# Wide products for forty blocks of the second gated layer and for the gated linear unit of the last mixer

## The chip, the core and the metric

The kernel is one program on one core of a Trainium2 chip. The metric is its time on the device in microseconds, as the median of several runs; a profiled execution stands beside it.

## What is computed

Two blocks of layers work on 256 tokens of width 2048. The first has two gated layers, the second four mixers (SSD, fox, MLA, S5), each with a layer norm behind it. The change touches the second gated layer and the last mixer. In the second gated layer (`last`), only keys and values are made for the 256 context tokens as well; everything else is for the 256 tokens alone:

```python
        proj = h @ w_in[layer]
        u, v_sgu, za, q, k, v, zb = jnp.split(proj, SPLIT_POINTS, axis=-1)
        q = apply_axial_rope(rms_norm(split_heads(q, N_Q_HEADS), q_norm_w[layer]), cos, sin)
        ...
        attn = blocked_gqa(q, k_all, v_all)
        sgu = chunk_sgu(u, v_sgu, w_sgu[layer], b_sgu[layer], v_norm_w[layer])
        y = jnp.concatenate([sgu * jax.nn.silu(za),
                             merge_heads(attn) * jax.nn.silu(zb)], axis=-1) @ w_out[layer]
```

The last mixer multiplies twice by a 2048 x 2048 matrix behind its state space part, the first time as a gated linear unit (GLU):

```python
    y = jax.nn.gelu(y)
    y = y * jax.nn.sigmoid(y @ w_glu.astype(f32) + b_glu.astype(f32))
    y = y * jax.nn.silu(z.astype(f32))
    return y.astype(h.dtype) @ w_out
```

## The kernel before

**Products in parts.** Every weight and every activation is split into a high part in the format of TensorE's quick float32 product and the low rest. A product of weight W and activation A is W_hi A_hi + W_hi A_lo + W_lo A_hi. The activations stand in `act_parts`, both parts of it, feature by feature (128 features to a tile, 256 tokens wide).

**The stream of weights.** Weights come from HBM in units of 128 x 1024 (8 tiles, 512 KB) through a ring of four (`raw`, `w_hi`, `w_lo`). SyncE starts the DMA of a unit as soon as TensorE has multiplied the unit four before it. ScalarE makes `w_hi` (line 510), VectorE `w_lo` (line 517), and TensorE waits for `w_lo` of a unit before its first tile.

**Blocks.** A `Block` makes 128 output features: 16 tiles, two units, into one PSUM bank. A narrow block has three products of 256 columns in a tile (lines 584, 586, 588). A wide block (`wide`) has two: line 581 multiplies the high weights with both parts of the activation at once, 512 columns, into both halves of the bank; line 588 adds the low weights' product to the first half. Somebody has to add the halves then. Where VectorE takes the result, it does so with one more add. Where ScalarE takes it, VectorE first adds the halves into `norm_root` (`add_halves`, line 620), and ScalarE takes from there. Before the change, all 65 input blocks of the fox mixer and 15 of the 16 output blocks of each mixer are wide; the gated layers, the MLA's and S5's input blocks and the GLU are narrow.

**The order.** `flow` writes out the instructions of a stage block by block, in slots. In slot g ScalarE and VectorE first split units until they are two units (`AHEAD`) past block g, with the side work of the stage in between or behind; then ScalarE takes block g. In the gated layers (`between` is true) the side work stands between the two units of a slot; in the S5 mixer both units come first and the side work behind them. Every engine works its queue in order, so an instruction that waits holds up all behind it.

**Second gated layer.** `LAYER_ORDER` gives the blocks: k, k, v, v, then q and zb of eight heads in turn, then vg and u of eight groups in turn, then eight za. Forty of them, all but k and v, have only the 256 tokens. The banks 0 and 1 take turns (`banks=2`). The attention of a head and the statistics of a group are side work of later slots.

**GLU.** Its 16 blocks follow the 32 input blocks of the S5 mixer. Of the first four the first halves (8 tiles) are multiplied ahead (`LEAD["s5_glu"]`), so that their own slots have one unit each. In a slot, behind the `w_lo`, VectorE does `gate` (line 3374) and `low_out` (3378) of the block before and `halve` (3369) of this one; ScalarE does `high_out` (3297) of the block before and then takes the block with a sigmoid (3442). `gate` waits for the take, `high_out` for `gate`, `low_out` for `high_out`:

```python
                if g - first_glu - 1 in range(KT - 1):
                    gate(dve, g - first_glu - 1)
                    low_out(dve, g - first_glu - 1)
                if g - first_glu in range(KT):
                    halve(dve, g - first_glu)
```

Of the kernel before, what the change touches and what calls it, by code (L numbers as in the profile page):

```python
# [19 lines left out]
KT = D // P  # L20
# [27 lines left out]
LEAD = dict(gate_in1=2, fox_in=3, mla_in=3, s5_in=2, s5_glu=4)  # L48
# [115 lines left out]
LAYER_ORDER = [(name, i) for name in "kv" for i in range(N_KV)] \  # L164
# [198 lines left out]
def halves_first(blocks, n):  # L363

    return [Part(block, block.kt // 2) for block in blocks[:n]] + blocks
# [7 lines left out]
def build(nc, ins, out):  # L373
    with ExitStack() as ctx:
# [304 lines left out]
        def act_rhs(width_of_block, offset=0, first=0):  # L679

            def rhs(k, part, w):
                a = (first + k) * width_of_block + offset
                return act_parts[:, part, a:a + w]
            return rhs
# [756 lines left out]
        def layer_flow(layer, before, behind):  # L1441

            last = layer == DEPTH - 1
# [492 lines left out]
            def wait_result(pe, kk):  # L1936
                if kk < 8:
                    pe.wait_ge(head_low.sem, head_low.at(kk + 1))
                else:
# [1 line left out]
            takes = dict(k=take_k, v=take_v, q=take_q, vg=take_vg, za=take_za, u=take_u, zb=take_zb)  # L1941
            blocks = [Block(KT, TT if name in "kv" else width, both, takes[name](i),
                            wait=None if (name, i) != LAYER_ORDER[0] else before.wait_tile,
                            shape=in_halves if last and name in "kv" else None) for name, i in LAYER_ORDER]
            for i in range(0 if last else QUARTERED):
                blocks[i].place = i
            blocks = halves_first(blocks, lead) if last else quarters_first(blocks, QUARTERED)
# [4 lines left out]

        first_input, second_input, tokens_in = FirstInput(), SecondInput(4, 5), Tokens()
        layer_flow(0, first_input, second_input)
        layer_flow(1, second_input, tokens_in)

        def add_scaled(dve, ps, b):
            if b == KT - 1:
                return dve.scalar_tensor_tensor(out=xT[:, b, :], in0=xT[:, b, :], scalar=ALPHA, in1=ps,
                                                op0=ALU.mult, op1=ALU.add)  # L1960
            ordered = order["vector"]
            dve.scalar_tensor_tensor(out=xT[:, b, :], in0=xT[:, b, :], scalar=ALPHA, in1=ps[:, 0, :],
                                     op0=ALU.mult, op1=ALU.add).then_inc(ordered.sem, 1)
            dve.wait_ge(ordered.sem, ordered.step())
            return dve.tensor_tensor(xT[:, b, :], xT[:, b, :], ps[:, 1, :], ALU.add)  # L1965
# [1164 lines left out]
        def s5():  # L3130
# [36 lines left out]
            last = KT - 1  # L3167
# [273 lines left out]
            def take_glu(b):  # L3441
                return lambda act, ps: act.activation(glu[:, b, :], ps, ACT.Sigmoid, bias=param("b_glu", b, b + 1))

            def wait_y(b):

                def wait(pe, kk):
                    if b == 2 and kk == 0:
                        pe.wait_ge(drive_read.sem, drive_read.at(KT))
                    if b == 0:
                        pe.wait_ge(y_low.sem, y_low.at(kk + 1))  # L3450
                return wait

            def wait_out(pe, kk):
# [2 lines left out]
                            wait=None if (name, k) != S5_ORDER[0] else norms[2].wait_tile) for name, k in S5_ORDER]  # L3456
            blocks = halves_first(blocks, lead)
            blocks += halves_first([Block(KT, T, act_rhs(T, first=KT), take_glu(b), wait=wait_y(b) if b in (0, 2) else None,
                                          place=(0, 1, 4, 5)[b] if b < 4 else None) for b in range(KT)], LEAD["s5_glu"])
            blocks += [Block(KT, T, act_rhs(T), lambda dve, ps, b=b: add_scaled(dve, ps, b), "dve",  # L3460
                             None if b else wait_out, wide=b < KT - 1) for b in range(KT)]
            norms.append(LayerNorm(3, 4, 5, out=False))
            flow(blocks, banks=2, before=norms[2], behind=norms[3], out_at=first_glu + KT, tensor_side=tensor_side, scalar_early=scalar_early, vector_side=vector_side,
                 gpsimd_side=gpsimd_side, scalar_first=scalar_first, vector_first=vector_first)
        s5()
        stage(tensor=norms[3].begin_tensor, scalar=lambda act: norms[3].begin_scalar(act, lambda i: None),
              vector=lambda dve: norms[3].begin_vector(dve, lambda i: None))
# [178 lines left out]
```

## Time and profile before

| | us |
|---|---|
| median of 3 runs | 3359.23 |
| lowest and highest | 3356.72, 3362.01 |
| profiled execution | 3363.07 |
| its span in the trace | 3360.9 |
| TensorE, VectorE, ScalarE busy | 3255.5, 2271.2, 1819.1 |

The span is what the trace covers; the execution has 2.2 us around it. Matmul ends are modelled, so distances are read from start to start. The second gated layer's forty blocks run from about 910 to 1189 us, the GLU's 16 blocks from about 3166 to 3247 us.

### The profile page before, as it was taken

What the parts mean: (1) busy time and instruction counts of PE and PEld (TensorE: products, weight loads), DVE (VectorE), ACT (ScalarE), POOL (GpSimd) and SP (SyncE); (2) the same over time, 40 slices, a digit from 0 to 9 for tenths busy, and PEclk for the clock granted to TensorE, in tenths of its full rate; (3) what the DMA queues carried; (4) which work ended last, traced back from release to release, by engine and by line L of the source; (5) the groups of instructions that cost most, each with busy time, mean ns of one, the idle gap of its engine ahead of it and who ended that gap; (6) DMA issues with size and microseconds to landing.
All of it is one profiled execution on the core that took longest, in us unless ns stands there. A gap on an engine that the chain in (4) does not pass through costs nothing.

```text
span 3360.9 us, 54980 instructions
## 1 busy us (share of the span) xinstructions
PE 3255.5 (97%) x22635; PEld 2905.6 (86%) x22635; DVE 2271.2 (68%) x3092; ACT 1819.1 (54%) x2888; POOL 482.2 (14%) x740
## 2 busy tenths in 40 slices
PE   7999999999899999999999999999999999899997
PEld 3688888788799999999999877888879998899996
DVE  2688889733555556766766676766676655899866
ACT  2344544232577646676775355555546564687644
POOL 0011111111000000000000014877120000322001
PEclk9999999999999999999999999999999999999999
DMA  9855566732244555555555546666545445455454
GB/s 344 286 184 182 181 210 221 285 111 94 84 136 151 176 182 190 195 182 199 184 187 166 184 151 197 219 217 208 178 158 167 148 135 177 150 170 168 158 183 143
DMA packets 175321, 608.44 MB, mean 181 GB/s; under 512 B 21888, under 2 KB 21920, under 8 KB 173408
## 3 DMA queue, kind: packets, MB, share of 16 engines
q1 hardware_dynamic: 145440, 495.54, 43.7%
q0 software_dynamic: 28624, 105.72, 9.1%
q8 instruction: 180, 2.95, 0.4%
q10 hardware_dynamic: 1008, 3.67, 0.3%
q14 instruction: 69, 0.57, 0.1%
HBM read 596.27 MB, written 8.57 MB: 180 GB/s over the span
## 4 chain that ended last, share of the span: by engine, by line
PE 83%; DVE 6%; ACT 4%; DMA 4%; issue 2%; SPq 0%; DVEq 0%; ACTq 0%
PE psum_all L588 24%; PE psum_all L584 18%; PE psum_all L586 18%; PE psum_all L581 12%; DMA raw<-in_stream 2%; DVE w_lo L517 2%; ACT w_hi L510 1%; DMA mod_early<-in_stream 1%; PE psum_all L1564 1%; PE psum_all L1531 1%; PE psum_all L751 1%; DMA mod_late<-in_stream 1%; DVE ln_d L1101 1%; PE psum_all L3202 1%; PE psum_all L3232 0%
## 5 line engine op out<-in xcount | busy, mean ns | idle before, releaser
L588 PE MATMUL psum_all<-act_parts,w_lo 128*128 128x256 f32 (+1 forms) x6704 | 2007.2, 299 | 0.0
L517 DVE TENSOR_TENSOR w_lo<-raw,w_hi 128x1024 fp32r<-128x1024 f32 x866 | 1071.7, 1245 | 704.6 <-ACT w_hi L510 702.3
L584 PE MATMUL psum_all<-act_parts,w_hi 128*128 128x256 f32 (+1 forms) x4464 | 1407.1, 315 | 37.3 <-DVE act_parts L978 13.8
L586 PE MATMUL psum_all<-act_parts,w_hi 128*128 128x256 f32 (+1 forms) x4464 | 1377.7, 309 | 0.0
L588 PEld LDWEIGHTS psum_all<-act_parts,w_lo 128*128 128x128 f32 x6704 | 1281.5, 191 | 41.5
L510 ACT ACTIVATE w_hi<-raw 128x1024 fp32r<-128x1024 f32 x866 | 911.9, 1055 | 687.2 <-DMA raw<-in_stream 685.4
L584 PEld LDWEIGHTS psum_all<-act_parts,w_hi 128*128 128x128 f32 x4464 | 856.4, 192 | 108.7 <-issue 43.3
L586 PEld LDWEIGHTS psum_all<-act_parts,w_hi 128*128 128x128 f32 x4464 | 857.5, 192 | 43.0 <-issue 3.4
L581 PE MATMUL psum_all<-act_parts,w_hi 128*128 128x512 f32 x2240 | 801.2, 402 | 14.6 <-DVE w_lo L517 7.1
L581 PEld LDWEIGHTS psum_all<-act_parts,w_hi 128*128 128x128 f32 x2240 | 422.5, 189 | 123.5 <-issue 10.3
L879 DVE SCALAR_TENSOR_TENSOR xT<-mod_late,small,xT 128x1024 f32<-128x1024 f32 x210 | 256.6, 1280 | 8.2 <-DMA mod_late<-in_stream 6.2
L814 POOL DMA_DIRECT2D mod_late<-in_stream x128 | 67.7, 529 | 568.2 <-DVE xT L879 375.6
L1072 POOL TENSOR_TENSOR ln_acc<-xT 128x256 f32<-128x256 f32 x8 | 5.9, 734 | 586.5 <-DVE xT L1965 586.5
L1072 POOL TENSOR_TENSOR ln_acc<-ln_acc,xT 128x256 f32<-128x256 f32 x44 | 48.2, 1095 | 222.3 <-DVE xT L1965 222.3
L751 PE MATMUL psum_all<-mod_early,s_silu 128*32 128x512 f32 x256 | 48.3, 678 | 24.9 <-DMA mod_early<-in_stream 24.7
L2382 DVE SCALAR_TENSOR_TENSOR conv_acc<-conv_x,params,conv_acc 128x255 f32<-128x255 f32 x144 | 69.3, 481 | 3.5
L1913 DVE SCALAR_TENSOR_TENSOR xT<-psum_all,modulation,xT 128x256 f32<-128x256 f32 x32 | 15.4, 483 | 81.5 <-PE psum_all L588 81.5
L2457 POOL DMA_DIRECT2D acs_rows<-ssd_acs x1 | 0.6, 556 | 467.3 <-DVE ssd_red L2374 467.3
L2462 POOL DMA_DIRECT2D ssd_seg<-acs_rows x8 | 4.3, 533 | 404.1 <-PE psum_all L2259 401.8
L2315 ACT ACTIVATE ssd_seg<-ssd_seg,ssd_src 128x128 f32<-128x128 f32 x192 | 58.6, 393 | 0.8 <-DMA ssd_seg<-acs_rows 0.8
L2471 ACT ACTIVATE conv_acc<-psum_all,params 128x256 f32<-128x256 f32 x48 | 27.0, 562 | 58.0 <-PE psum_all L588 57.4
L751 PEld LDWEIGHTS psum_all<-mod_early,s_silu 128*32 128x32 f32 x256 | 8.2, 115 | 51.0 <-DMA mod_early<-in_stream 35.7
(499 smaller groups left out, 3398.4 us busy)
## 6 DMA issues: line engine op xcount, KB each, us to landing
raw<-in_stream SPq DMA_DIRECT2D x858, 512.0 KB, 3.3
mod_late<-in_stream POOLq DMA_DIRECT2D x128, 512.0 KB, 4.2
mod_early<-in_stream SPq DMA_DIRECT2D x128, 256.0 KB, 6.3
ssd_seg<-acs_rows POOLq DMA_DIRECT2D x8, 1536.0 KB, 6.6
s_matrices<-s5p_made POOLq DMA_DIRECT2D x16, 384.0 KB, 3.0
raw<-in_stream SPq DMA_DIRECT2D x16, 256.0 KB, 5.1
s_made<-s_matrices POOLq DMA_DIRECT2D x16, 256.0 KB, 3.0
xT<-in_x SPq DMA_DIRECT2D x1, 2048.0 KB, 10.5
```

Of the source, the lines that this page charges most:

```text
L510: act.activation(w_hi[:, n % RING, :], raw[:, n % RING, :], ACT.Copy).then_inc(hi_ready, 1)
L517: dve.tensor_tensor(w_lo[:, n % RING, :], raw[:, n % RING, :], w_hi[:, n % RING, :].bitcast(F32), ALU.subtract).then_inc(lo_ready, 1)
L581: pe.matmul(block.both, w_hi[:, n % RING, cols], block.rhs(kk, BOTH, block.width), start=(kk == 0), stop=False)
L584: pe.matmul(sums, w_hi[:, n % RING, cols], block.rhs(kk, HIGH, block.width), start=(kk == 0), stop=False)
L586: pe.matmul(sums, w_hi[:, n % RING, cols], block.rhs(kk, LOW, block.width), start=False, stop=False)
L588: last = pe.matmul(sums, w_lo[:, n % RING, cols], block.rhs(kk, HIGH, block.width), start=False, stop=(kk == block.kt - 1))
L751: last = pe.matmul(bank[rows, :], s_silu[:, k, :], early_units[early_slot(m)][:, h * 512:(h + 1) * 512], start=(k < 2), stop=(k >= KT - 2))
L814: pool.dma_start(late_units[:, m % LATE_RING, :], ins["stream"][u]).then_inc(late_landed[m % LATE_RING], 16)
L879: dve.scalar_tensor_tensor(out=sums, in0=unit, scalar=s_late[:, k, v:v + 1], in1=sums, op0=ALU.mult, op1=ALU.add).then_inc(late_summed, 1)
L1072: pool.tensor_tensor(acc, acc if b % 8 > 1 else xT[:, b - 1, :], xT[:, b, :], ALU.add) \
L2315: one = act.activation(s, s, ACT.Relu, bias=src_cum[:, g * HG + j, k:k + 1], scale=-1.0)
L2382: dve.scalar_tensor_tensor(out=conv_acc[i % 2][:, back:T], in0=conv_x[i % 2][:, 0:T - back], scalar=conv_col(block, tap), in1=conv_acc[i % ...
```

## The change

The forty blocks without context of the second gated layer and the 16 blocks of the GLU become wide:

```diff
@@ -1941,7 +1941,8 @@
                             wait=None if (name, i) != LAYER_ORDER[0] else before.wait_tile,
-                            shape=in_halves if last and name in "kv" else None) for name, i in LAYER_ORDER]
+                            shape=in_halves if last and name in "kv" else None,
+                            wide=last and name not in "kv") for name, i in LAYER_ORDER]
@@ -3456,7 +3457,7 @@
             blocks += halves_first([Block(KT, T, act_rhs(T, first=KT), take_glu(b), wait=wait_y(b) if b in (0, 2) else None,
-                                          place=(0, 1, 4, 5)[b] if b < 4 else None) for b in range(KT)], LEAD["s5_glu"])
+                                          place=(0, 1, 4, 5)[b] if b < 4 else None, wide=True) for b in range(KT)], LEAD["s5_glu"])
```

Lines behind the first place move down by one (3374 becomes 3375).

TensorE has 896 instructions less. This is a piece of the difference, at the start of the forty blocks, behind a transpose of v (L1506) and a rotation of k (L1499); rows that repeat are left out:

```order
 L1499 MATMUL psum_all<-k_6455,consts 128x256
-L584 MATMUL psum_all<-act_parts,w_hi 128x256
-L586 MATMUL psum_all<-act_parts,w_hi 128x256
-L588 MATMUL psum_all<-act_parts,w_lo 128x256
...
+L581 MATMUL psum_all<-act_parts,w_hi 128x512
+L588 MATMUL psum_all<-act_parts,w_lo 128x256
```

Each tile has one product of 512 columns where it had two of 256.

VectorE in the second gated layer, behind the rotation of the first head's q (L1734, L1736) and at its row maxima (L1758, L1763):

```order
 L1734 TENSOR_TENSOR q_6454<-q_6454,consts 128x256
 L1736 TENSOR_TENSOR q_6454<-q_6454,qk_spin_6462 128x256
-L517 TENSOR_TENSOR w_lo<-raw,w_hi 128x1024 x3
+L517 TENSOR_TENSOR w_lo<-raw,w_hi 128x1024 x2
+L620 TENSOR_REDUCE norm_root<-psum_all 128x256
+L517 TENSOR_TENSOR w_lo<-raw,w_hi 128x1024
 L1758 TENSOR_REDUCE head_stat_0_6463<-psum_all 128x1 x2
 L1763 SCALAR_TENSOR_TENSOR head_stat_0_6463<-head_stat_0_6463 128x2
 L517 TENSOR_TENSOR w_lo<-raw,w_hi 128x1024
+L620 TENSOR_REDUCE norm_root<-psum_all 128x256
```

An add of the halves stands behind the last `w_lo` of each slot.

VectorE in the GLU, between two blocks in its middle, before:

```order
L3369 TENSOR_TENSOR s_z<-s_z,s_u 128x256 [waits taken_by_scalar]
L517 TENSOR_TENSOR w_lo<-raw,w_hi 128x1024 [waits hi_ready] x2
L3374 TENSOR_TENSOR s_glu<-s_glu,s_z 128x256 [waits s5_halved,taken_by_scalar]
L3378 TENSOR_TENSOR act_parts<-s_glu,act_parts 128x256 [waits s5_high2]
L3369 TENSOR_TENSOR s_z<-s_z,s_u 128x256 [waits taken_by_scalar]
```

and after:

```order
L3370 TENSOR_TENSOR s_z<-s_z,s_u 128x256 [waits taken_by_scalar]
L620 TENSOR_REDUCE norm_root<-psum_all 128x256 [waits taken_by_scalar,multiplied]
L517 TENSOR_TENSOR w_lo<-raw,w_hi 128x1024 [waits hi_ready] x2
L3375 TENSOR_TENSOR s_glu<-s_glu,s_z 128x256 [waits s5_halved,taken_by_scalar]
L3379 TENSOR_TENSOR act_parts<-s_glu,act_parts 128x256 [waits s5_high2]
```

The add stands behind gate, split and halve, ahead of the next two `w_lo`. ScalarE's order is the same as before; in the GLU its take (L3442, now L3443) waits for `halves_added` where it waited for `multiplied`, and reads `norm_root` where it read PSUM.

## Rows read from the trace of the kernel before

**Rows 1.** The page's busy time, share of the span and instructions of each engine.
```profile
PE 3255.5 (97%) x22635; PEld 2905.6 (86%) x22635; DVE 2271.2 (68%) x3092; ACT 1819.1 (54%) x2888; POOL 482.2 (14%) x740
```

**Rows 2.** Windows, layer and GLU: busy us (count) of PE, PEld, DVE, ACT, POOL; clock.
```profile
910.00:1189.00 279.00, 279.00 (x2193) 269.18 (x2193) 146.51 (x226) 190.48 (x300) 0.00 (x0) 1.00 0.47 155
3166.00:3247.00 81.00, 81.00 (x685) 80.81 (x674) 51.27 (x75) 41.27 (x60) 0.00 (x0) 1.00 0.53 178
```

**Rows 3.** Timeline of TensorE in the GLU: start, duration, engine, line, operation.
```profile
3176.00 0.28 PE L584 MATMUL psum_all<-act_parts,w_hi 128*128 128x256 f32 x1
...
3178.88 0.28 PE L584 MATMUL psum_all<-act_parts,w_hi 128*128 128x256 f32 x1
```

**Rows 4.** Timeline of TensorE in two output projections with wide tiles.
```profile
2803.66 0.39 PE L581 MATMUL psum_all<-act_parts,w_hi 128*128 128x512 f32 x1
...
2809.21 0.39 PE L581 MATMUL psum_all<-act_parts,w_hi 128*128 128x512 f32 x1
...
3246.92 0.40 PE L581 MATMUL psum_all<-act_parts,w_hi 128*128 128x512 f32 x1
...
3252.57 0.40 PE L581 MATMUL psum_all<-act_parts,w_hi 128*128 128x512 f32 x1
```

**Rows 5.** Timeline of VectorE, then ScalarE, at a halves-add of the fox mixer.
```profile
2102.06 0.68 DVE L620 TENSOR_REDUCE norm_root<-psum_all 128x256 f32<-128x512 f32 x1
...
2102.77 0.42 ACT L2826 ACTIVATE fox_q<-norm_root 128x256 f32<-128x256 f32 x1 [1.91 <-DVE norm_root L620]
2103.09 1.04 ACT L510 ACTIVATE w_hi<-raw 128x1024 fp32r<-128x1024 f32 x1
```

**Rows 6.** Timeline of VectorE in the second gated layer (vg slot, za slots).
```profile
1096.89 1.23 DVE L517 TENSOR_TENSOR w_lo<-raw,w_hi 128x1024 fp32r<-128x1024 f32 x1
...
1175.17 1.23 DVE L517 TENSOR_TENSOR w_lo<-raw,w_hi 128x1024 fp32r<-128x1024 f32 x1 [1.00 <-ACT w_hi L510]
1178.02 1.23 DVE L517 TENSOR_TENSOR w_lo<-raw,w_hi 128x1024 fp32r<-128x1024 f32 x1 [1.62 <-ACT w_hi L510]
```

**Rows 7.** Timeline of ScalarE in the same slots.
```profile
1092.22 0.38 ACT L1902 ACTIVATE u<-psum_all 128x256 f32<-128x256 f32 x1 [1.44 <-PE psum_all L588]
...
1098.64 0.38 ACT L1891 ACTIVATE vg<-psum_all 128x256 f32<-128x256 f32 x1 [0.48 <-PE psum_all L588]
...
1176.57 0.38 ACT L1898 ACTIVATE za<-psum_all 128x256 f32<-128x256 f32 x1 [1.43 <-PE psum_all L588]
...
1179.85 1.06 ACT L510 ACTIVATE w_hi<-raw 128x1024 fp32r<-128x1024 f32 x1 [1.55 <-DMA raw<-in_stream]
```

**Rows 8.** Timeline of VectorE in the GLU: block 0, then block 14.
```profile
3169.88 0.42 DVE L3369 TENSOR_TENSOR s_z<-s_z,s_u 128x256 f32<-128x256 f32 x1
...
3239.95 1.22 DVE L517 TENSOR_TENSOR w_lo<-raw,w_hi 128x1024 fp32r<-128x1024 f32 x1 [1.10 <-ACT w_hi L510]
3241.09 0.42 DVE L3374 TENSOR_TENSOR s_glu<-s_glu,s_z 128x256 f32<-128x256 f32 x1
3241.99 0.43 DVE L3378 TENSOR_TENSOR act_parts<-s_glu,act_parts 128x256 fp32r<-128x256 f32 x1 [0.48 <-ACT act_parts L3297]
3242.33 0.42 DVE L3369 TENSOR_TENSOR s_z<-s_z,s_u 128x256 f32<-128x256 f32 x1
3243.30 1.23 DVE L517 TENSOR_TENSOR w_lo<-raw,w_hi 128x1024 fp32r<-128x1024 f32 x1 [0.55 <-ACT w_hi L510]
```

**Rows 9.** Timeline of ScalarE in the GLU at block 14.
```profile
3241.54 0.42 ACT L3297 ACTIVATE act_parts<-s_glu 128x256 fp32r<-128x256 f32 x1 [1.63 <-DVE s_glu L3374]
3241.86 0.46 ACT L3442 ACTIVATE s_glu<-psum_all,params 128x256 f32<-128x256 f32 x1
3242.22 1.05 ACT L510 ACTIVATE w_hi<-raw 128x1024 fp32r<-128x1024 f32 x1
```

**Rows 10.** Timeline of TensorE at the start of the fox mixer.
```profile
1998.46 0.76 PE L581 MATMUL psum_all<-act_parts,w_hi 128*128 128x512 f32 x1 [4.92 <-DVE act_parts L1158]
```

**Rows 11.** Busy time and granted clock just behind it (columns as in rows 2).
```profile
1999.00:2010.00 11.00, 8.80 (x26) 6.39 (x24) 10.93 (x18) 9.61 (x17) 0.00 (x0) 0.50 0.15 48
```

## The prediction

> **What bounds the kernel now.** I read first the busy shares of the page: TensorE is busy 97% of the span, VectorE 68%, ScalarE 54% [rows 1]. An average doesn't tell what a single stage waits for, so the windows come next: in the second gated layer (910 to 1189 us) TensorE is busy 279.0 of 279 us and VectorE 146.5; in the gated linear unit, GLU below (3166 to 3247), TensorE is busy 81.0 of 81 us, VectorE 51.3, and the clock is 1.00 (2.4 GHz) in both [rows 2]. So both changed stretches go by the rhythm of TensorE's products. But VectorE and ScalarE make the weight halves for them, in program order, in the same queues in which they take the results. So the third view is the timeline of the three engines: what a tile costs TensorE, and how much of a block's time the other two need.
>
> **What a tile costs.** A narrow tile is three products of 256 columns. In the GLU its first product starts at 3176.00 and that of the tile eight later at 3178.88 [rows 3]: 0.360 us a tile, 5.76 us a block of 16. A wide tile (512 and 256 columns) is in this kernel already. Sixteen of them take 3246.92 to 3252.57 us, 0.353 each, and sixteen others 2803.66 to 2809.21, 0.347 each [rows 4]. These are two rhythms that a stretch keeps from its first product on; in the timelines about four tiles in five go by the slower. I take 0.352, so a changed tile gives TensorE 0.008 us; the bounds are 0.0067 and 0.013.
>
> A page of the Trainium skill would give less. "TensorE: Matmul & The Clock Gate", section "Back-to-back issue gap", puts a warm product at its columns through 2.4 GHz plus 2.5 ns, so that two of 256 cost 218 ns and one of 512 costs 216, and a tile would win 0.0026 us. Row and rule disagree here: by the rule a narrow tile is 0.328 us, and the trace has 0.360.
>
> **Second gated layer: 40 blocks, 640 tiles.** TensorE saves 640 x 0.008 = 5.1 us (4.3 to 8.3). Added are 40 halves-adds on VectorE (line 620). One takes 0.68 us, and ScalarE's take starts 0.71 us after the add began, its next instruction 0.32 us after that [rows 5]. 40 x 0.68 = 27 us fit into the 132 us in which VectorE is idle there, so throughput is no question. The order is: VectorE now stands at the add until the block's last product, and ScalarE stands at its take until the add is through; behind them wait the next w_hi and w_lo. In a za block nothing but its 16 tiles is on TensorE. There w_lo starts at 1175.17 and ends at 1176.40, the take starts at 1176.57 and the next w_lo at 1178.02 [rows 6, 7]. The add goes in at about 1176.5, and take, w_hi and w_lo move by some 0.7 us: that w_lo ends at 1179.95. TensorE wants it one block after 1176.4, at 1182.0, so 2 us are left. The second w_hi (1179.85) waits for its DMA, and by then ScalarE is free again: nothing is handed on. The tightest are the vg and u pairs, where ScalarE makes statistics between u's take (1092.22) and the second w_lo (1096.89), the last thing before vg's add: 4.67 + 1.14 + 0.71 = 6.5 us from take to take, where the trace has 6.42 (1098.64) [rows 6, 7]. That hands on 0.1 to 0.3 us, and the u slot behind it, which has no statistics, takes it back. A q and zb pair has TensorE's attention work beside its tiles, so more room. Banks: with two of them, a block needs the bank of the last but one, whose take is late by 0.7 us and has 5.65. I put the loss in the layer at 0, at most 1 us.
>
> **GLU: 16 blocks, 256 tiles.** Here the order is another: in each slot both w_lo come first, then gate, split and halve of the block before (lines 3374, 3378, 3369), and now the add behind these. The steps form a ring over the two engines, read from the starts [rows 8, 9]: last w_lo to gate 1.14 (3239.95 to 3241.09), gate to ScalarE's split 0.45 (3241.54), split to VectorE's 0.45 (3241.99), to halve 0.34 (3242.33). From there on before ScalarE did not wait for it: the take started 0.32 after its split (3241.86), w_hi 0.36 after that (3242.22), w_lo 1.08 later (3243.30), and the second w_lo could follow 1.14 later. The ring before is 1.14 + 0.45 + 0.32 + 0.36 + 1.08 + 1.14 = 4.5 us with two units a slot, under TensorE's 5.76.
> Now the take hangs behind split, halve and add: 1.14 + 0.45 + 0.45 + 0.34 + 0.35 (halve to add) + 0.71 + 0.32 + 1.08 + 1.14 = 5.98 us, over the 5.65 of TensorE; with one unit 4.84, where TensorE takes 2.83. The ring becomes the bound.
> Its start: halve at 3169.88, add 3170.23, take 3170.94, w_hi 3171.26, w_lo 3172.34. Blocks 0 to 3 have one unit each left when their slots come, so the next w_lo come at 3177.2 and 3182.0, and from 3186.8 on, with two units a slot, every 5.98 us: the w_lo of the first output block is eleven slots on, 3252.6. Block 4 began at 3177.80, five tiles after 3176.00 [rows 3]; TensorE now reaches it at 3177.6 and finds its w_lo ready at 3178.4: waits of 0.8, 2.0 and 2.0 us, then 0.3 in each block.
> At the end, block 15 has gate and split in front of the next w_hi: second w_lo 1.14, gate 1.14, split 0.45 and 0.45, halve 0.34, add 0.35, take 0.71, gate 0.46, split 0.45, w_hi 0.33, w_lo 1.08 make 6.9 us: that w_lo starts at 3259.5 and ends at 3260.7. Before, TensorE began this block at 3252.57 [rows 4], without a wait. So the GLU ends 8.1 us later; I take 8.0. Each 0.1 us by which the ring is off gives 1.5 us in its 15 rounds: bounds 6.5 and 9.5. The GLU's own saving of 256 x 0.008 = 2.0 us is in this and comes out as waiting.
>
> **The sum.** 8.0 - 5.1 = +2.9 us. The profiled execution took 3363.07 us (span 3360.9 and 2.2 around it), so it would be 3366.0. It lies 3.8 over the median of the three runs, 3359.23, to which the prediction refers: 3362.1 us. By the page's price of a tile the layer would give 1.7 instead of 5.1.
>
> **The rivals.**
> TensorE stays the bound in both stretches: the ring is shorter than I read it, as an add might start beside the halve, or the take beside a split. Then 896 x 0.008 = 7.2 us are gained: 3352.0. For it: the ring must lose only 0.33 us. Against: it needs 2 us more at blocks 0 to 3, and each step is a start-to-start distance from a row.
> The layer gets a ring too (slower). Place: its 40 blocks; the 0.7 us handed on grows from block to block once the chain add, take, w_hi, w_lo and the side work between passes 5.65 us. At the GLU's 0.3 us a block it costs 13 us and the saving there is gone by it: 3362.1 + 13 = 3375. Against: in za the chain is 5.1 us, and the idle time of the windows.
> The clock falls in the GLU. At 1999 to 2010 us TensorE ran at 0.50 (1.2 GHz), after an idle time of 4.92 us [rows 10, 11]; the waits of 2.0 us between units of 2.83 could do it. At that level the 8 x 768 columns of a unit take 5.1 us, over the ring's 4.84 and, twice in a slot, over its 5.98; for some 11 us this adds about 5: 3367.
> The tile is cheaper by less than the rows say. A wide tile behind attention work could cost what the page's rule says, 0.0026 us under a narrow one: 640 x 0.0026 = 1.7 us, so 3365.5. Against: both rhythms of the trace save at least 0.0067.
> That the change doesn't do what it says is excluded by the order: 896 products are gone and 56 adds are there.
>
> **How the numbers follow.** Forecast with its own bounds (-1.8 to +6.2): 3357 to 3365.5, chance 0.62. TensorE stays the bound 0.12, ring in the layer 0.10, clock 0.08, cheaper by less 0.08. The range of 3354 to 3369 leaves out the first and the third of these five and little else. A measurement tells 0.2%, 6.7 us, from no change: faster is under 3352.5, slower over 3365.9. Half of the second case and a tail of the first are faster, 0.10; the ring in the layer, most of the clock case and the upper tail of the forecast are slower, 0.24; the rest, 0.66, is within.
>
> **What would show it.** In the profile after, line 581 has 2240 + 896 = 3136 products, lines 584 and 586 have 3568 each. The second layer ends 4 to 8 us earlier, counted from its start, with TensorE still without waits. In the GLU takes are 4.8 us apart in the first four blocks and 6.0 then, TensorE waits for w_lo some 9 us in all, in about 15 places, and VectorE's stand in front of w_lo is on w_hi. If TensorE's waits there are under 2 us, or if line 620 is followed by w_lo waits in the layer, I am wrong.

## The result, and the profile after

The kernel before takes 3356.12 us (median of 20 runs, 3353.37 to 3362.01), the changed one 3360.41 us (median of 20, 3356.84 to 3367.36). The ratio is 1.0014, with a 95% interval of 1.0007 to 1.0020: 4.7 us slower (the medians differ by 4.3), which lies within the 0.2% that I named as no change. The forecast was 3362.1 us, 2.9 over before. The three runs from which it set out had a median 3.1 us above that of the twenty; I compare ratios and stages from here on, not totals.

The page of the changed kernel, engines and the two lines that the forecast counts on (line, engine, operation, tiles, count; busy us and mean ns; idle us before them and its main releaser):

```profile
PE 3244.4 (97%) x21739; PEld 2851.9 (85%) x21739; DVE 2302.7 (69%) x3148; ACT 1820.0 (54%) x2888; POOL 483.1 (14%) x740
...
L581 PE MATMUL psum_all<-act_parts,w_hi 128*128 128x512 f32 x3136 | 1121.8, 402 | 21.6 <-DVE w_lo L517 13.9
...
L620 DVE TENSOR_REDUCE norm_root<-psum_all 128x256 f32<-128x512 f32 x121 | 82.7, 683 | 5.9 <-PE psum_all L588 5.4
```

Against [rows 1] there are 896 products less and 56 adds more, and line 581 has its 3136. The average hides what happened: TensorE has fewer busy microseconds, and the time is not shorter. The windows of the two changed stretches (busy us and count of PE, PEld, DVE, ACT, POOL; clock, DMA share, GB/s) show where it stands:

```profile
910.00:1185.00 275.00, 273.89 (x1559) 234.62 (x1558) 171.28 (x267) 189.59 (x300) 0.00 (x0) 1.00 0.47 158
3159.00:3246.00 87.00, 79.77 (x439) 66.55 (x438) 56.84 (x87) 39.54 (x57) 0.00 (x0) 1.00 0.50 167
```

In [rows 2] TensorE was busy in the whole of both. Now it lacks 1.1 us in the layer and 7.2 us in the GLU. TensorE's waits from 3150 to 3260 us (us in total, times, longest), in the view of waits:

```profile
PE psum_all L581 <- DVE w_lo L517: 8.2, 14, 1.9
```

and in the layer (908 to 1186 us), where before had none:

```profile
PE psum_all L581 <- DVE w_lo L517: 0.7, 1, 0.7
PE psum_all L1531 <- ACT probs L1631: 0.4, 1, 0.4
```

For every kernel I measured the stages between fixed places of its timeline: the layer from its last rotation of k on TensorE (L1499) to the take of its first output block on VectorE, the GLU from the last small product of the S5 scan to the take of the first output block behind it. One profiled execution each, in us (everything else is the span less the two); ratios are to before, with their 95% interval:

| kernel | layer | GLU | everything else | ratio |
|---|---|---|---|---|
| before | 283.9 | 87.9 | 2989.1 | |
| after | 279.7 | 97.4 | 2980.7 | 1.0014 (1.0007 to 1.0020) |
| GLU alone wide | 283.9 | 97.4 | 2983.1 | 1.0029 (1.0021 to 1.0038) |
| layer alone wide | 279.5 | 87.5 | 2980.9 | 0.9986 (0.9977 to 0.9995) |
| before, a sum beside | 285.1 | 87.8 | 2981.0 | 1.0000 (0.9992 to 1.0009) |
| before, the sum in the ring | 284.0 | 97.2 | 2984.0 | 1.0027 (1.0016 to 1.0039) |
| GLU blocks 0 to 3 wide | 284.1 | 94.6 | 2984.3 | 1.0020 (1.0011 to 1.0029) |
| GLU blocks 4 to 15 wide | 283.9 | 91.7 | 2984.9 | 1.0008 (0.9998 to 1.0017) |
| both wide, GLU's add first | 279.6 | 89.3 | 2981.6 | 0.9994 (0.9985 to 1.0002) |
| layer and GLU 4 to 15 wide, add first | 279.4 | 86.5 | 2982.7 | 0.9979 (0.9970 to 0.9988) |

The changed layer is 4.3 us shorter, the changed GLU 9.5 us longer: +5.2, beside the 4.7 of the ratio. The fourth column is code that no kernel here changes, and still it differs by up to 8.4 us. That is why the profiled execution of after (3359.99 us, span 3357.8) is shorter than that of before (3363.07), against the sign of the medians; the last section comes back to it.

The ring itself, in the profile after. VectorE in the middle of the GLU (start, duration, engine, line, operation; idle before it and who ended it; x2 are two `w_lo` in a row):

```profile
3236.69 2.36 DVE L517 TENSOR_TENSOR w_lo<-raw,w_hi 128x1024 fp32r<-128x1024 f32 x2 [1.53 <-ACT w_hi L510]
3238.97 0.42 DVE L3375 TENSOR_TENSOR s_glu<-s_glu,s_z 128x256 f32<-128x256 f32 x1
3239.87 0.42 DVE L3379 TENSOR_TENSOR act_parts<-s_glu,act_parts 128x256 fp32r<-128x256 f32 x1 [0.48 <-ACT act_parts L3298]
3240.22 0.42 DVE L3370 TENSOR_TENSOR s_z<-s_z,s_u 128x256 f32<-128x256 f32 x1
3240.55 0.68 DVE L620 TENSOR_REDUCE norm_root<-psum_all 128x256 f32<-128x512 f32 x1
3242.76 2.36 DVE L517 TENSOR_TENSOR w_lo<-raw,w_hi 128x1024 fp32r<-128x1024 f32 x2 [1.53 <-ACT w_hi L510]
```

and ScalarE beside it:

```profile
3239.42 0.42 ACT L3298 ACTIVATE act_parts<-s_glu 128x256 fp32r<-128x256 f32 x1 [1.81 <-DVE s_glu L3375]
3241.27 0.51 ACT L3443 ACTIVATE s_glu<-norm_root,params 128x256 f32<-128x256 f32 x1 [1.43 <-DVE norm_root L620]
3241.68 1.99 ACT L510 ACTIVATE w_hi<-raw 128x1024 fp32r<-128x1024 f32 x2
```

One round is 3242.76 - 3236.69 = 6.07 us. From start to start: two `w_lo` 2.28, gate to split 0.45, to split low 0.45, to halve 0.35, to the add 0.33, to the take 0.72, to `w_hi` 0.41, to `w_lo` 1.08. No engine is busy in all of it: VectorE stands 1.53 us at `w_hi`, ScalarE 1.43 us at the add. In [rows 9] the take followed its split by 0.32 us and waited for no one; here it comes 1.85 us behind it (3239.42 to 3241.27). TensorE at the starts of the blocks, where products wait:

```profile
3167.53 0.47 PE L581 MATMUL psum_all<-act_parts,w_hi 128*128 128x512 f32 x1 [0.97 <-DVE w_lo L517]
3172.37 0.50 PE L581 MATMUL psum_all<-act_parts,w_hi 128*128 128x512 f32 x1 [1.78 <-DVE w_lo L517]
3177.39 0.47 PE L581 MATMUL psum_all<-act_parts,w_hi 128*128 128x512 f32 x1 [1.94 <-DVE w_lo L517]
3183.45 0.47 PE L581 MATMUL psum_all<-act_parts,w_hi 128*128 128x512 f32 x1 [0.27 <-DVE w_lo L517]
3189.52 0.47 PE L581 MATMUL psum_all<-act_parts,w_hi 128*128 128x512 f32 x1 [0.19 <-DVE w_lo L517]
```

That is the forecast's picture: 0.8, 2.0 and 2.0 us, then some 0.3 a block.

### The profile page after: what moved, and what is told of

Its sections match the earlier page's. It is cut to its first block, busy times and chain, and to the rows that moved or that the text cites. A ratio compares the mean times of both kernels' runs of the same rounds, so it can differ in the third digit from the quotient of the medians.

```text
span 3357.8 us, 53300 instructions
## 1 busy us (share of the span) xinstructions
PE 3244.4 (97%) x21739; PEld 2851.9 (85%) x21739; DVE 2302.7 (69%) x3148; ACT 1820.0 (54%) x2888; POOL 483.1 (14%) x740
## 4 chain that ended last, share of the span: by engine, by line
PE 80%; DVE 8%; ACT 6%; DMA 4%; issue 2%; SPq 0%; DVEq 0%; ACTq 0%
PE psum_all L588 23%; PE psum_all L581 17%; PE psum_all L584 15%; PE psum_all L586 14%; DVE w_lo L517 3%; DMA raw<-in_stream 2%; ACT w_hi L510 2%; DMA mod_early<-in_stream 1%; PE psum_all L1531 1%; PE psum_all L1564 1%; PE psum_all L751 1%; DMA mod_late<-in_stream 1%; DVE ln_d L1101 1%; DVE xT L879 0%; PE psum_all L2259 0%
## 5 line engine op out<-in xcount | busy, mean ns | idle before, releaser
L584 PE MATMUL psum_all<-act_parts,w_hi 128*128 128x256 f32 (+1 forms) x3568 | 1146.8, 321 | 38.5 <-DVE act_parts L978 14.4
L581 PE MATMUL psum_all<-act_parts,w_hi 128*128 128x512 f32 x3136 | 1121.8, 402 | 21.6 <-DVE w_lo L517 13.9
L586 PE MATMUL psum_all<-act_parts,w_hi 128*128 128x256 f32 (+1 forms) x3568 | 1122.9, 315 | 0.0
L584 PEld LDWEIGHTS psum_all<-act_parts,w_hi 128*128 128x128 f32 x3568 | 683.5, 192 | 107.9 <-issue 38.7
L581 PEld LDWEIGHTS psum_all<-act_parts,w_hi 128*128 128x128 f32 x3136 | 590.1, 188 | 173.9 <-issue 21.5
L586 PEld LDWEIGHTS psum_all<-act_parts,w_hi 128*128 128x128 f32 x3568 | 684.1, 192 | 40.8 <-issue 1.4
L620 DVE TENSOR_REDUCE norm_root<-psum_all 128x256 f32<-128x512 f32 x121 | 82.7, 683 | 5.9 <-PE psum_all L588 5.4
```

The lines of the kernel that those rows point to most:

```text
L581: pe.matmul(block.both, w_hi[:, n % RING, cols], block.rhs(kk, BOTH, block.width), start=(kk == 0), stop=False)
L584: pe.matmul(sums, w_hi[:, n % RING, cols], block.rhs(kk, HIGH, block.width), start=(kk == 0), stop=False)
L586: pe.matmul(sums, w_hi[:, n % RING, cols], block.rhs(kk, LOW, block.width), start=False, stop=False)
L620: dve.reduce_sum(norm_root[:, :], block.both.rearrange("p v t -> p t v"), AX_X).then_inc(halves_added, 1)
```

## The experiments

My theory: the GLU loses because ScalarE's take hangs behind VectorE's add, so that the two engines' steps form a ring of 6 us over TensorE's 5.65; the layer wins the tiles' saving. Rivals: TensorE itself is slower with wide tiles in the GLU; the 16 adds cost by their work alone; the layer loses too.

### One part alone

The GLU alone, from after:

```diff
-                            wide=last and name not in "kv") for name, i in LAYER_ORDER]
+                            wide=False) for name, i in LAYER_ORDER]
```

> Only the GLU's 16 blocks are wide, the second gated layer is as before. Ring theory (the take hangs behind gate, split, halve and add, and the two engines go round in 4.9 us with one unit and 6.07 us with two): the GLU, from its first own product to the second output block's first, takes 9.5 us more than before, TensorE waits for w_lo some 8 to 9 us there, and the time is before + 9 us, ratio 1.0027. Rival (the time after comes from the layer, not the GLU): ratio within 0.1% of 1.

The layer alone, from after:

```diff
-                                          place=(0, 1, 4, 5)[b] if b < 4 else None, wide=True) for b in range(KT)], LEAD["s5_glu"])
+                                          place=(0, 1, 4, 5)[b] if b < 4 else None) for b in range(KT)], LEAD["s5_glu"])
```

> Only the forty blocks of the second gated layer are wide, the GLU is as before. If a changed tile gives 0.0067 us or a little more and one collision of 1 us at the change from heads to groups stays: the layer takes 4 us less, ratio 0.9988 (time before - 4 us). Rival (the adds in the layer hold up the queues and eat the gain, as the late takes of q in the trace could suggest): ratio 1.0000 or above. With the GLU-only kernel the two differences must sum to that of the whole change, +4.7 us.

Measured: 3366.35 us for the GLU alone and 3351.44 for the layer alone, beside 3356.36 of before. The ratios are +9.7 and -4.7 us, +5.0 together, and after has +4.7. The parts add up, and the layer pays for half of what the GLU costs. A ring in the layer is refuted: alone it is faster, its interval wholly under 1.

### Is it the add's work, or that the take waits for it?

Both kernels keep all products narrow, as before, and give VectorE a sum in each of the 16 GLU blocks, at the add's place and of its size. It reads two halves of `act_parts` in SBUF, not the bank, and nobody needs its result. In the first nobody waits for it; in the second ScalarE's take does. (The field `extra`, set in the 16 GLU blocks, and its counting are left out here.)

```diff
-                    if taken_by(g, "act") and blocks[g].wide:
+                    if taken_by(g, "act") and (blocks[g].wide or blocks[g].extra):
```

```diff
-                dve.reduce_sum(norm_root[:, :], block.both.rearrange("p v t -> p t v"), AX_X).then_inc(halves_added, 1)
+                pair = act_parts[:, :, KT * T:KT * T + T].bitcast(F32) if block.extra else block.both
+                dve.reduce_sum(norm_root[:, :], pair.rearrange("p v t -> p t v"), AX_X).then_inc(halves_added, 1)
```

and in the second kernel also, on ScalarE, ahead of its wait for `halves_added`:

```diff
-                        if blocks[g].wide:
+                        if blocks[g].wide or blocks[g].extra:
```

> The kernel before, all blocks of the GLU narrow; VectorE makes at the place of the add a sum of the same size, from SBUF, that nobody uses, and ScalarE's take doesn't wait for it. Ring theory: VectorE has 0.35 to 0.68 us more in each slot, but the take stays beside it and w_hi starts as before: the takes stay 3.35 and 5.76 us apart, the GLU takes 0 to 0.5 us more, ratio 1.0000. Rival (it is VectorE's time for the add that costs): the GLU takes 8 to 10 us more, ratio 1.0026.

> As the kernel with the unused sum, but ScalarE's take waits for it, as it does for the add of a wide block. No product is wide. Ring theory: the takes are 4.9 and 6.0 us apart, TensorE waits for w_lo 7 to 8 us in the GLU (0.1 us a block less than with wide tiles, since it is itself slower), and the GLU ends as late as with wide blocks: 8.5 to 9.5 us more than before, ratio 1.0027. Rival (wide products or the add's reading of PSUM beside them slow TensorE in the GLU): ratio within 0.1% of 1.

Measured: 1.0000 (0.9992 to 1.0009) and 1.0027 (1.0016 to 1.0039), GLU 87.8 and 97.2 us. This is the cleanest result of the study: not one wide product, and the whole loss is there. VectorE and ScalarE in the middle of the GLU, the sum beside:

```profile
3202.61 0.70 DVE L622 TENSOR_REDUCE norm_root<-act_parts 128x256 f32<-128x512 f32 x1
...
3201.49 0.42 ACT L3299 ACTIVATE act_parts<-s_glu 128x256 fp32r<-128x256 f32 x1 [1.63 <-DVE s_glu L3376]
3201.81 0.46 ACT L3444 ACTIVATE s_glu<-psum_all,params 128x256 f32<-128x256 f32 x1
```

and the sum in the ring:

```profile
3205.61 0.70 DVE L622 TENSOR_REDUCE norm_root<-act_parts 128x256 f32<-128x512 f32 x1
...
3204.48 0.42 ACT L3299 ACTIVATE act_parts<-s_glu 128x256 fp32r<-128x256 f32 x1 [1.81 <-DVE s_glu L3376]
3206.35 0.48 ACT L3444 ACTIVATE s_glu<-psum_all,params 128x256 f32<-128x256 f32 x1 [1.45 <-DVE norm_root L622]
```

The sum takes 0.70 us in both. Beside, the take starts 0.32 us behind its split and ahead of the sum; in the ring it starts 1.87 us behind the split. The 1.45 us in which ScalarE stands idle ahead of its take, in the last row, show the mechanism.

I was wrong on how the waiting would look: I expected 7 to 8 us of listed waits of TensorE, and the view lists 4.2 (3.0 in four, 1.2 in one). With narrow tiles a block needs 5.76 us of the ring's 6.05, so each wait is under 0.3 us, and the view doesn't mark such short ones: product starts at block edges stand 0.35 us apart (3202.78 to 3203.13) where 0.12 is usual. The length of the stage is the safer measure.

### Which blocks pay

Layer narrow in both; from after:

```diff
-                                          place=(0, 1, 4, 5)[b] if b < 4 else None, wide=True) for b in range(KT)], LEAD["s5_glu"])
+                                          place=(0, 1, 4, 5)[b] if b < 4 else None, wide=b < 4) for b in range(KT)], LEAD["s5_glu"])
```

and `wide=b >= 4` in the other.

> Of the GLU only the first four blocks are wide, those with one unit left in their own slot; all else is as before. Ring theory: four rounds of 4.9 us where TensorE needs 2.9 for a unit, then narrow blocks without a loss: the GLU takes 4.8 us more than before (92.7 where before has 87.9), ratio 1.0014. Rival (each wide block costs the same 0.6 us, 9.5 over 16): 2.4 us more.

> Of the GLU only the last twelve blocks are wide, those with two units in their slot; all else is as before. Ring theory: takes 6.07 us apart from the fifth block on, starting with the lead in w_lo that the first four narrow blocks leave: the GLU takes 3.8 us more (91.7), ratio 1.0011. With the first four it sums to 8.6 of the 9.5. Rival (the same for each wide block): 7.1 us more.

Blocks 4 to 15: 91.7 us, +3.8 on the point, ratio 1.0008. Blocks 0 to 3: 94.6, +6.7 where +4.8 was expected, ratio 1.0020. The takes show that the ring did as computed in blocks 0 to 3 (4.94, 4.93 and 4.94 us apart, where before has 3.37, 3.35 and 3.36). What was missing in my sum is on TensorE, right behind the third wait (timeline of TensorE, GLU with blocks 0 to 3 wide):

```profile
3182.52 0.28 PE L588 MATMUL psum_all<-act_parts,w_lo 128*128 128x256 f32 x1
3184.69 0.54 PE L584 MATMUL psum_all<-act_parts,w_hi 128*128 128x256 f32 x1 [1.89 <-DVE w_lo L517]
3185.03 0.41 PE L586 MATMUL psum_all<-act_parts,w_hi 128*128 128x256 f32 x1
...
3188.02 0.33 PE L584 MATMUL psum_all<-act_parts,w_hi 128*128 128x256 f32 x1
```

Products start 0.21 us apart, where they are 0.12 apart before and after. Windows of the same kernel, behind the wait and after that (columns as above, the third number from the end is the granted clock):

```profile
3184.70:3188.00 3.30, 3.30 (x15) 3.30 (x16) 2.27 (x5) 1.96 (x4) 0.00 (x0) 0.50 0.27 109
3188.10:3192.00 3.90, 3.90 (x34) 3.90 (x34) 3.16 (x5) 1.04 (x2) 0.00 (x0) 1.00 0.39 133
```

The clock was at 0.50 (1.2 GHz) for 3.3 us, behind idle times of 0.97, 1.74 and 1.89 us. The 16 tiles from 3184.69 take 7.33 us (to 3192.02) where 16 take 5.76: 1.57 us lost, which with the 4.8 is 6.4 of the 6.7. So the rival on the clock was real, as an addition, in this execution. (The ratio's interval, 1.0011 to 1.0029, holds the expected 1.0014 too, so it doesn't tell in how many of the ten runs the clock fell.) Without this loss blocks 0 to 3 cost 5.1 us, and with the 3.8 of the other twelve that is 8.9 of the 9.5. In the GLU alone wide the clock fell too:

```profile
3181.00:3183.80 2.80, 2.71 (x9) 1.91 (x8) 1.28 (x2) 2.27 (x3) 0.00 (x0) 0.50 0.00 0
```

(the stretch before it, 3177 to 3180.5, has 1.00), but there it cost nothing: the GLU is 97.38 us long, and 97.35 in after, whose profiled execution has the same products and waits and keeps 1.00 throughout. Wide blocks follow there, bound by the ring, and the slower unit only ate its own wait (0.68 us at 3184.39, where after has 1.94). In these two traces the low clock cost time where TensorE set the pace, and none where TensorE waited anyway.

### Can the add leave the ring?

In the ring the add waits behind gate, split and halve, with which it has nothing to do. Here VectorE does it ahead of them, right behind the slot's `w_lo`; from after, and `early=True` at the GLU's blocks:

```diff
+                    early = taken_by(g, "act") and blocks[g].early
+                    if early:
+                        add_halves(dve, blocks[g], ends[g] + 1)
                     if vector_side:
                         vector_side(dve, g)
...
-                    if taken_by(g, "act") and blocks[g].wide:
+                    if taken_by(g, "act") and blocks[g].wide and not early:
```

> The whole change, but in the GLU VectorE makes the halves-add of a block ahead of gate, split and halve, not behind them. Ring theory: the round becomes last w_lo to add 1.14, add to gate 0.65, to ScalarE's split 0.45, take 0.33, w_hi 0.33, w_lo 1.08 and, with two units, 1.14: 4.0 and 5.1 us, so TensorE waits some 2 us in the first blocks and not in the later twelve. The GLU takes 0 to 1 us more than before (88 to 89), with the layer's -4.4 the time is before - 4, ratio 0.9989. Rival (an add before each take costs its 0.7 us wherever it stands): GLU +9, ratio 1.0014 as the whole change.

The last one keeps blocks 0 to 3 of the GLU narrow, in which even this ring is longer than TensorE's unit:

```diff
-                                          place=(0, 1, 4, 5)[b] if b < 4 else None, wide=True) for b in range(KT)], LEAD["s5_glu"])
+                                          place=(0, 1, 4, 5)[b] if b < 4 else None, wide=b >= 4, early=b >= 4) for b in range(KT)], LEAD["s5_glu"])
```

> The layer wide as in the change, of the GLU only the last twelve blocks, their adds ahead of gate, split and halve. Ring theory: no round is longer than what TensorE needs; the GLU takes 1.3 us less than before (192 tiles x 0.0067; 86.6), with the layer's -4.4 the time is before - 5.7, ratio 0.9983, the fastest of all. Rival (wide products in the GLU gain nothing): GLU 87.9, ratio 0.9987.

Measured: GLU 89.3 us where 88 to 89 was expected, and 86.5 where 86.6 was; ratios 0.9994 (0.9985 to 1.0002) and 0.9979 (0.9970 to 0.9988). TensorE's waits with all blocks wide are 0.77 and 1.04 us in the first blocks, about as computed, and 0.50 us at 3203.26, for which the ring alone gives no reason. It begins with a transfer: the DMA of one unit took 5.3 us from issue to landing there (3191.48 to 3196.78), where the others of the stretch mostly take 3.1 to 3.4. VectorE, then ScalarE, with the add first (the kernel with all blocks wide):

```profile
3204.17 0.68 DVE L621 TENSOR_REDUCE norm_root<-psum_all 128x256 f32<-128x512 f32 x1
3204.77 0.41 DVE L3379 TENSOR_TENSOR s_glu<-s_glu,s_z 128x256 f32<-128x256 f32 x1
3205.66 0.43 DVE L3383 TENSOR_TENSOR act_parts<-s_glu,act_parts 128x256 fp32r<-128x256 f32 x1 [0.48 <-ACT act_parts L3302]
3206.01 0.42 DVE L3374 TENSOR_TENSOR s_z<-s_z,s_u 128x256 f32<-128x256 f32 x1
3207.01 2.36 DVE L518 TENSOR_TENSOR w_lo<-raw,w_hi 128x1024 fp32r<-128x1024 f32 x2 [0.59 <-ACT w_hi L511]
...
3205.21 0.42 ACT L3302 ACTIVATE act_parts<-s_glu 128x256 fp32r<-128x256 f32 x1 [2.41 <-DVE s_glu L3379]
3205.54 0.49 ACT L3447 ACTIVATE s_glu<-norm_root,params 128x256 f32<-128x256 f32 x1
3205.94 1.99 ACT L511 ACTIVATE w_hi<-raw 128x1024 fp32r<-128x1024 f32 x2
```

The take has no idle time in front of it again and starts 0.33 us behind the split. A round is 5.12 us, under TensorE's 5.65. With the first four narrow, TensorE has no wait left in the GLU:

```profile
3157.00:3244.00 87.00, 87.00 (x526) 76.73 (x523) 63.69 (x96) 45.96 (x66) 0.00 (x0) 1.00 0.54 179
```

At 3348.89 us (3346.71 to 3352.66 in 11 runs) it is the fastest kernel here, and by its ratio 0.2% faster than before, where the whole change is 0.14% slower; over the layer alone (0.9986) its lead is inside the intervals, and rests on the GLU's 1.0 us.

## Why the prediction was right

**GLU, +8.0 forecast, +9.5 measured.** The mechanism was right step by step: ring over TensorE, large waits at three of the first blocks, small ones behind. The term that was mis-sized is the ring's round: 5.98 forecast, 6.07 measured, and 4.93 where 4.84 was forecast. It is one step: take to `w_hi`, for which I took 0.32 us from a plain copy in the fox mixer [rows 5], although [rows 9] had 0.36 for the GLU's own take and I used that in the ring before; the sigmoid's take from `norm_root` lasts 0.51 us and its successor follows 0.41 behind. In 15 rounds 0.09 us make 1.35 of the 1.5 us. The bounds of 6.5 to 9.5, built on just this, held, but only just. TensorE's listed waits are 8.2 us in 14 places, where I wrote some 9 in about 15.

**Layer, -5.1 forecast, -4.3 measured** (-4.4 alone). Two things that partly cancel. The tiles gave more than my 0.008 us each: in the trace some 45% of them go by the quicker rhythm, not one in five, for which 640 x 0.0097 = 6.2 us would be due. And "TensorE still without waits" was wrong: the step that failed is the loss that I put at 0. It is 1.1 us by the view of waits and 1.5 by the starts of products: at 941.37, where the view has 0.37 us, 2.27 us pass from one tile to the next (1.68 before), and at 1059.37, where it has 0.74, 1.25 us pass where tiles in a row stand 0.35 apart. So the tiles gave some 5.8 us (4.3 + 1.5), and 0.4 of the 6.2 stay open. By its own last sentence the prediction was wrong in the layer: a wait for `w_lo` came there beside line 620.

My reading by slots, za and the vg and u pairs, was right: the takes of u and vg stand 6.34 us apart (1089.65 to 1095.99), with no wait on TensorE. I had not read the one place where the last head's statistics meet the first group. The profile after there (ScalarE, VectorE, TensorE by time):

```profile
1049.70 1.06 ACT L510 ACTIVATE w_hi<-raw 128x1024 fp32r<-128x1024 f32 x1 [0.15 <-DMA raw<-in_stream]
...
1055.21 1.28 ACT L1682 ACT_TABLE_LOAD   x1
...
1058.08 1.28 ACT L1891 ACT_TABLE_LOAD   x1
1058.09 1.22 DVE L517 TENSOR_TENSOR w_lo<-raw,w_hi 128x1024 fp32r<-128x1024 f32 x1 [0.52 <-ACT w_hi L510]
1059.23 0.68 DVE L620 TENSOR_REDUCE norm_root<-psum_all 128x256 f32<-128x512 f32 x1
...
1059.37 0.51 PE L581 MATMUL psum_all<-act_parts,w_hi 128*128 128x512 f32 x1 [0.74 <-DVE w_lo L517]
1059.95 0.42 ACT L1891 ACTIVATE vg<-norm_root 128x256 f32<-128x256 f32 x1 [0.59 <-DVE norm_root L620]
```

and before:

```profile
1052.44 1.06 ACT L510 ACTIVATE w_hi<-raw 128x1024 fp32r<-128x1024 f32 x1 [1.09 <-DMA raw<-in_stream]
...
1060.83 1.23 DVE L517 TENSOR_TENSOR w_lo<-raw,w_hi 128x1024 fp32r<-128x1024 f32 x1 [0.52 <-ACT w_hi L510]
```

Two table loads and the statistics stand between ScalarE's halves there, but they are no longer than before: from the first `w_hi` to the `w_lo` it is 8.39 us in both (1049.70 to 1058.09, 1052.44 to 1060.83). Before, this `w_lo` ended at 1062.06 and the first tile that needs it started at 1062.20, so 0.14 us were left; a TensorE that gets there sooner uses them up. The rest goes with the start of the chain, which in both is the landing of a unit's DMA. It landed 4.34 us after its issue before and 4.98 after, where most units of the layer take 3.1 to 3.5; ScalarE's two small loads, `w_sgu` and `b_sgu`, are on their way then. In the four kernels with a wide layer it took 4.74, 4.97, 4.98 and 5.21 us, and TensorE waited 0.43, 0.74, 0.74 and 0.97 us; in the six with a narrow one it took 4.28 to 4.63 us, and the view lists no wait (by the starts of products, 0.2 and 0.3 us are lost there in the two at 4.51 and 4.63).

So the table loads didn't grow, and no add lies in the chain behind this landing. Why the DMA takes longer in the four, and whether the small loads slow it, no experiment took apart. The other wait, of 0.37 us, is the attention's product waiting for the softmax of a head: from the table load ahead of the statistics on ScalarE to this product it is 5.59 us after (935.78 to 941.37), and 6.02 before (936.99 to 943.01), where TensorE came later and waited for nothing.

**Sum and range.** +2.9 forecast, +4.7 measured by the ratio, both errors on the same side; 3354 to 3369 held it. That 3362.1 lies only 1.7 over the measured 3360.41 is luck: the median of three from which it started is 3.1 us over that of the twenty, and this hid the 1.8 by which the change itself was forecast too small. The two cases that the range leaves out are TensorE as the bound (3352.0) and the ring in the layer (3375), the second and third of the five and not "the first and the third" as I wrote.

**The rivals.** TensorE bound in both: refuted by the 8.2 us of waits. It comes near the truth for the order that the last experiment has (0.9979 is 7.0 us, where it had 7.2). A ring in the layer: refuted by the layer alone. The clock in the GLU: it fell in three of the profiled executions with such waits (GLU alone, blocks 0 to 3, sum in the ring) and not in after's. I had priced 11 us at low clock and 5 us of time; the runs show 3 us at low clock, and a loss of 0 where the ring was the bound and 1.6 in narrow blocks that TensorE bounds. The tile cheaper by less: refuted, since 640 tiles at 0.0026 (0.0025 without rounding on the way) give 1.7 us and the layer alone is 4.4 us shorter, in spite of its waits. (Its ratio alone, up to 0.9995, would just allow 1.7.) The Trainium skill's rule for a warm product ("TensorE: Matmul & The Clock Gate", section "Back-to-back issue gap") gives that price, and the measurement decides against it here. That page of the Trainium skill offers the rule for an isolated product, which the prediction doesn't say, and not for a stream in which each product has its own weight load, as here (21739 products and 21739 loads).

## What to carry to other kernels

Moving work from a full engine to an idle one costs nothing only if nobody's order comes to hang on it: here 11 us of adds on an engine with room cost nothing as a sum beside, and cost 9 us as soon as a take on a second engine waited for them, since that take stood ahead of the operands for the first. Before such a change, write the chain from one operand to the next through all engines' queues, from start to start, and compare it with the time that the full engine needs for the same piece; do it for the shortest pieces and the seams between phases too. If the chain is the longer one, look first for a step in it that needs nothing from its neighbours, and put it where the engine is idle anyway. Read too where each unit's DMA lands, since a chain can start there: the wait in the layer and the late one with the add first both began with a landing 4.7 to 5.3 us behind its issue.

## What the runs showed of the hardware that I had not expected

**Two rhythms, each kept until the next break.** Sixteen wide tiles, timeline of TensorE in the profile after, twice in the layer and once in the last output projection:

```profile
1137.58 0.39 PE L581 MATMUL psum_all<-act_parts,w_hi 128*128 128x512 f32 x1
1143.22 0.40 PE L581 MATMUL psum_all<-act_parts,w_hi 128*128 128x512 f32 x1
...
1149.32 0.40 PE L581 MATMUL psum_all<-act_parts,w_hi 128*128 128x512 f32 x1
1154.86 0.40 PE L581 MATMUL psum_all<-act_parts,w_hi 128*128 128x512 f32 x1
...
3251.54 0.39 PE L581 MATMUL psum_all<-act_parts,w_hi 128*128 128x512 f32 x1
3257.08 0.39 PE L581 MATMUL psum_all<-act_parts,w_hi 128*128 128x512 f32 x1
```

5.64, 5.54 and 5.54 us: 0.353, 0.346 and 0.346 a tile. In [rows 4] the last stage, whose code is the same in both kernels, went at 0.353. In the SSD mixer's output projection, unchanged too, before has 14 tiles at the quick rhythm and 456 at the slow one, after 123 and 346. It is not drawn at random for each stretch, though: in the four kernels with a wide layer the first 17 unbroken stretches of the layer have the same rhythm in all four executions, and they differ from the eighteenth on. A thousand tiles by one or the other are 6.7 us, more than this whole change moves. What picks the rhythm stays open.

**A short low clock.** Short idle times of TensorE in the GLU went ahead of about 3 us at 1.2 GHz in three executions: 0.97 and 1.82 us with the GLU alone wide, 0.71 and 1.72 with the sum in the ring, 0.97, 1.74 and 1.89 with blocks 0 to 3 wide. In after 0.97, 1.78 and 1.94 us of idle time had no such effect, so the same waits don't always bring it. At that level products of 256 columns start 0.21 us apart; at 2.4 GHz they are not twice as quick but 0.12 apart.

**What single executions differ by.** The fourth columns of before and after differ by 8.4 us. The rhythm explains about 1 us of it: outside the changed stretches after has some 140 tiles more at the quick one. The clock is a second part. At the forty-first `w_lo` (360 us) before is already 1.7 us behind after, and 2.7 to 4.2 behind four other kernels whose code up to there is the same; TensorE stood at 0.50 for 11.7 us of this stretch in before, for 0 to 3 in the others. The rest comes in small pieces over the whole timeline, and its cause stays open.
